# Moving the rotation of queries and keys of a two-layer attention block from VectorE to GpSimd

## The reference

```python
qa = rope_2d(rmsnorm(qa.reshape(B, S, A_HEADS, HEAD_DIM), q_norm_a[e]), grid_row, grid_col)
ka = rope_2d(rmsnorm(ka.reshape(B, S, A_KV, HEAD_DIM), k_norm_a[e]), grid_row, grid_col)
ya = global_gqa(qa, ka, va.reshape(B, S, A_KV, HEAD_DIM))

def rmsnorm(x, g):            # y = x * rsqrt(mean(x*x) + EPS) * g
def _rotate_axis(xa, ang):    # x1, x2 = halves of 16: [x1*c - x2*s, x1*s + x2*c]
```

## Time and profile before

| | us |
|---|---|
| median of 3 runs | 2544.85 |
| lowest and highest | 2544.52, 2552.52 |
| the profiled execution, its own time | 2547.12 |
| its span, first to last instruction | 2545.3 |
| TensorE busy | 2409.3 |
| VectorE busy | 1325.8 |
| ScalarE busy | 1209.5 |
| GpSimd busy | 864.6 |

### The profile page before, as it was taken

How to read it: one execution, slowest core, us unless ns; L and a number is a source line. 1 busy time by engine, 2 the same in 40 slices (tenths; PEclk the granted TensorE clock), 3 DMA queues, 4 the chain that set the end, 5 groups by cost and what they waited for, 6 DMA issues and landing times.

```text
span 2545.3 us, 36154 instructions
## 1 busy us (share of the span) xinstructions
PE 2409.3 (95%) x12568; PEld 2029.2 (80%) x12568; DVE 1325.8 (52%) x2734; ACT 1209.5 (48%) x2873; POOL 864.6 (34%) x1063
## 2 busy tenths in 40 slices
PE   7999888999999999999999999998899999999999
PEld 6878677878887878888888887776678888888877
DVE  7444667666776423345655555676766303322321
ACT  6444455556675434455656555554554213322331
POOL 5433111111225642221222222567665323222322
PEclk9999999999999999999999999999999999999999
DMA  6312101111234242222222323422233211111112
GB/s 216 111 55 67 30 26 26 30 36 32 62 93 127 85 132 63 88 70 86 87 79 81 88 87 120 142 75 76 70 87 94 66 49 46 49 50 47 50 50 87
DMA packets 305844, 191.92 MB, mean 75 GB/s; under 512 B 63744, under 2 KB 284160, under 8 KB 305152
## 3 DMA queue, kind: packets, MB, share of 16 engines
q1 hardware_dynamic: 305664, 189.61, 25.2%
HBM read 170.16 MB, written 19.40 MB: 74 GB/s over the span
## 4 chain that ended last, share of the span: by engine, by line
PE 79%; DVE 9%; issue 5%; ACT 4%; POOL 3%; DMA 1%; SPq 0%; DVEq 0%; POOLq 0%; ACTq 0%
PE PS L1464 21%; PE PS L1466 20%; PE PS L1465 20%; PE PS L1610 5%; PE PS L1577 4%; PE PS L1564 2%; PE PS L1565 2%; PE PS L1621 2%; POOL WS L2295 1%; ACT PY L1699 1%; DVE ST L2046 1%; ACT PT L1699 1%; DVE PY L2120 1%; ACT EO L1699 1%; DVE QKV L1920 1%
## 5 line engine op out<-in xcount | busy, mean ns | idle before, releaser
L2295 POOL TENSOR_TENSOR WS<-WR,WS 128x256 fp32r<-128x256 f32 (+1 forms) x939 | 726.2, 792 | 1565.9 <-ACT WS L1699 1564.8
L1464 PE MATMUL PS<-HT,WS 128*128 128x512 f32 x2080 | 839.3, 404 | 37.2 <-POOL WS L2295 18.0
L1466 PE MATMUL PS<-HT,WS 128*128 128x512 f32 x2080 | 816.9, 393 | 0.0
L1465 PE MATMUL PS<-HT,WS 128*128 128x512 f32 x2080 | 816.5, 393 | 0.0
L1699 ACT ACTIVATE WS<-WR 128x256 fp32r<-128x256 f32 (+1 forms) x954 | 355.3, 408 | 375.4 <-PE PS L1466 342.8
L1464 PEld LDWEIGHTS PS<-HT,WS 128*128 128x128 f32 x2080 | 394.7, 190 | 134.2 <-issue 33.3
L1466 PEld LDWEIGHTS PS<-HT,WS 128*128 128x128 f32 x2080 | 393.9, 189 | 84.7
L1465 PEld LDWEIGHTS PS<-HT,WS 128*128 128x128 f32 x2080 | 395.2, 190 | 74.4
L1699 ACT ACTIVATE PT<-PS 128x512 fp32r<-128x512 f32 x352 | 186.1, 529 | 242.8 <-PE PS L1577 242.4
L1920 DVE TENSOR_TENSOR PT<-PS,PT 128x512 fp32r<-128x512 f32 x352 | 208.4, 608 | 92.1 <-ACT PT L1699 90.8
L1610 PE MATMUL PS<-PT,QKV 128*128 128x256 f32 (+1 forms) x1248 | 210.9, 291 | 12.5 <-DVE YB L2110 11.7
(11 more groups left out here) (176 smaller groups left out, 2908.1 us busy)
## 6 DMA issues: line engine op xcount, KB each, us to landing
WR<-in_ffn_in SPq DMA_DIRECT2D x120, 256.0 KB, 2.9
WR<-in_w_in_odd SPq DMA_DIRECT2D x106, 256.0 KB, 3.0
EO<-in_grid SPq DMA_DIRECT2D x48, 384.0 KB, 3.1
WR<-in_w_in_even SPq DMA_DIRECT2D x100, 128.0 KB, 2.6
WR<-in_w_out_odd SPq DMA_DIRECT2D x48, 256.0 KB, 2.9
yd<-PY SPq DMA_DIRECT2D x44, 256.0 KB, 3.2
WR<-in_w_in_even SPq DMA_DIRECT2D x34, 256.0 KB, 2.9
WR<-in_w_out_even SPq DMA_DIRECT2D x64, 128.0 KB, 2.8
```

Source lines behind the costliest of these rows:

```text
L1464: e.matmul(out, wh, rh, start=start, stop=False)
L1465: e.matmul(out, wh, rl, start=False, stop=False)
L1466: return e.matmul(out, wl, rh, start=False, stop=stop)
L2295: e.tensor_tensor(WS[:, i % NSPL, 1, 0:n], RAW[raw_slot(u)][:, o:o + n], f32(WS[:, i % NSPL, 0, 0:n]), ALU.subtract).then_inc(s_wlop.sem, 1)
```

## The change

Rope 2 and rope 3 are dealt out anew. GpSimd makes, as rope 2, all that was in either except for the product with the root: gain, four sine products, cosines, sum, seven operations on a semaphore of its own (`s_rp`). VectorE keeps the sum of squares (rope 1) and, as rope 3, makes the product with the root, which now comes last. F1 is free after GpSimd's first operation. Rope 3 is put one yield later. GpSimd makes the root of rope 1 first, as before, since that stands ahead in the list.

```diff
             yield False
-            h.vd2 = s_ed.n
-            s_ed.add(6)
-            f1["after"] = (s_ed, h.vd2 + 1)
+            h.vp2 = s_rp.n
+            s_rp.add(7)
+            f1["after"] = (s_rp, h.vp2 + 1)
             put("rope 2", h)
             at["f1"] = False
             yield False
-            h.vd3 = s_ed.n
-            s_ed.add(2)
+            yield False
+            h.vd3 = s_ed.add()
             put("rope 3", h)
             yield True
...
                 elif kind == "rope 4":
                     h, = of
-                    w.wait_ge(s_ed, h.vd3 + 2)
+                    w.wait_ge(s_ed, h.vd3)
...
-                elif kind == "rope 2":
...
                 elif kind == "rope 3":
                     h, = of
-                    a4 = RA.rearrange("p (t h f) -> p t h f", t=4, h=2)
-                    w.wait_ge(s_ed, h.vd2 + 6)
-                    e.tensor_tensor(a4, a4, COS[:, 4 * h.n:4 * h.n + 4, :].unsqueeze(2).to_broadcast([128, 4, 2, 64]), ALU.mult).then_inc(s_ed.sem, 1)
-                    w.wait_ge(s_ed, h.vd3 + 1)
-                    e.tensor_tensor(RA, RA, RBUF, ALU.add).then_inc(s_ed.sem, 1)
+                    a3 = RA.rearrange("p (g f) -> p g f", f=64)
+                    w.wait_ge(s_rs, h.vp)
+                    w.wait_ge(s_rp, h.vp2 + 7)
+                    e.tensor_tensor(a3, a3, SS[:, 8:16].unsqueeze(2).to_broadcast([128, 8, 64]), ALU.mult).then_inc(s_ed.sem, 1)
...
+                elif kind == "rope 2":
+                    h, = of
+                    gi = h.to[4]
+                    a3, x3 = RA.rearrange("p (g f) -> p g f", f=64), F1[:, :].rearrange("p (g f) -> p g f", f=64)
+                    w.wait_ge(s_ea, h.va + 2)
+                    w.wait_ge(s_ed, h.vd + 1)
+                    w.wait_ge(d_tab, 64)
+                    e.tensor_tensor(a3, x3, GQ[:, gi:gi + 1, :].to_broadcast([128, 8, 64]), ALU.mult).then_inc(s_rp.sem, 1)
...
+                    w.wait_ge(s_rp, h.vp2 + 1)
+                    for hh in range(2):
+                        for s in range(2):
+                            e.tensor_tensor(b5[:, :, hh, :, s, :], a5[:, :, hh, :, 1 - s, :], t5[:, :, :, s, :], ALU.mult).then_inc(s_rp.sem, 1)
+                    w.wait_ge(s_rp, h.vp2 + 5)
+                    e.tensor_tensor(a4, a4, COS[:, 4 * h.n:4 * h.n + 4, :].unsqueeze(2).to_broadcast([128, 4, 2, 64]), ALU.mult).then_inc(s_rp.sem, 1)
+                    w.wait_ge(s_rp, h.vp2 + 6)
+                    e.tensor_tensor(RA, RA, RBUF, ALU.add).then_inc(s_rp.sem, 1)
```

More of the change, by code:

```diff
@@ L277, in build @@
         s_whi, s_wlop, s_wlov, s_wused = (signal(n) for n in ("s_whi", "s_wlop", "s_wlov", "s_wused"))
-        s_mm, s_ea, s_ed, s_flip, s_rs = (signal(n) for n in ("s_mm", "s_ea", "s_ed", "s_flip", "s_rs"))
+        s_mm, s_ea, s_ed, s_flip, s_rs, s_rp = (signal(n) for n in ("s_mm", "s_ea", "s_ed", "s_flip", "s_rs", "s_rp"))
         s_score, s_mx, s_exp, s_sink, s_rec = (signal(n) for n in ("s_score", "s_mx", "s_exp", "s_sink", "s_rec"))
@@ L2310, in gpsimd_program @@
                     root(SS, 0, 8, 8).then_inc(s_rs.sem, 1)
+                elif kind == "rope 2":
[6 more added lines that the diff above has]
+                    e.tensor_tensor(a3, x3, GQ[:, gi:gi + 1, :].to_broadcast([128, 8, 64]), ALU.mult).then_inc(s_rp.sem, 1)
+                    a5 = RA.rearrange("p (t h x s f) -> p t h x s f", t=4, h=2, x=2, s=2)
+                    b5 = RBUF.rearrange("p (t h x s f) -> p t h x s f", t=4, h=2, x=2, s=2)
+                    t5 = SIN[:, 4 * h.n:4 * h.n + 4, :].rearrange("p t (x s f) -> p t x s f", x=2, s=2)
+                    a4 = RA.rearrange("p (t h f) -> p t h f", t=4, h=2)
+                    w.wait_ge(s_rp, h.vp2 + 1)
[6 more added lines that the diff above has]
+                    e.tensor_tensor(RA, RA, RBUF, ALU.add).then_inc(s_rp.sem, 1)
                 elif kind == "nsplit lo":
```

## The result

| | before | changed |
|---|---|---|
| median of the runs, us | 2548.71 (5 runs, 2544.52 to 2552.52) | 2535.14 (5 runs, 2531.48 to 2536.05) |
| the profiled execution, its own time | 2547.12 | 2536.05 |
| its span | 2545.3 | 2534.2 |

The ratio is 0.9946, with a 95% interval of 0.993 to 0.9963: 13.6 us or 0.54% faster in the medians, 11.1 us in the two profiled executions. Forecast were 2535 us and a gain of 9.7 us. So the time came out as forecast while the gain was some 4 us larger than forecast, and the base some 4 us higher: two misses that cancel.

The account below looks back on a forecast made before the run. TensorE holds 79% of the chain, so time lies only in its idle or lower-clock stretches. 7.1 + 5.7 - 2.8 - 0.3 = 9.7 us gained, giving 2535 us from the median 2544.85; 8-in-10 range 2530 to 2547.

Parts of the forecast that it names:

- The price on GpSimd: Seven rotation operations in each half, priced like GpSimd's subtractions: 5.7 us, 5.9 with three handovers.
- The warning end: GpSimd's power, 1.64 us for 8 columns, kept only as a warning that the operations might cost more than subtractions.
- Part 1: Global attention, six halves q05:0 to q07:1: rotation leaves VectorE's queue ahead of the score's maximum; 7.1 us gained.
- the cover of the kept product: Global attention: VectorE's 0.69 us product fits in 1.03 us before the exponential starts; without cover 0.7 us each.
- Part 2: ka:1: v's turning passes rope 4, removing waits of 2.22 and 4.26 us; net 5.7 us gained.
- 2.0 us of half clock: ka:1: TensorE's slow stretch at 191 to 198 us goes with the waits, worth 2.0 us.
- Part 3: q04:1: TensorE waits for rope 1 to 4, GpSimd's longer chain counting 1:1; 2.8 us lost.
- (c): Rival: TensorE's clock falls elsewhere; longer q04:1 hole keeps 6 us more at half clock, 3 us lost; chance 0.12.
- Part 4: ka:0 and q04:0, beside memory attention: low parts covered by 1.3 and 0.2 us; 0.3 us lost before q04:0's rope 4.
- (a): Rival: GpSimd operations cost more than subtractions, nearly 4 us per us over 5.9; no gain at 1.5 times; chance 0.18.
- (b): Rival: passing in ka:1 doesn't pay, the 4.26 us only move; gain there 2 us or less; chance 0.15.
- (d): Rival: more comes back than counted, VectorE also leaving rope 3's turn (1.8 us each); 2529 to 2531; chance 0.07.

Follow-up runs that it names:

- e10: Changed kernel without the extra step, GpSimd also making the product with the root as eighth operation: 2542.12 us, ratio 0.9974 to before.
- e2: Changed kernel without the extra step, rope 3 at its old place: 2554.51 us, ratio 1.0033 to before.
- e12: Changed kernel unchanged, run again on the chip of the versions it is compared with: 2535.31 us, ratio 0.9943 to before.
- e5: Only q05, q06 and q07 rotated the new way, ka and q04 as in the kernel before: 2537.29 us, ratio 0.9955 to before.
- e7: Changed kernel with one more 512-column operation in GpSimd's chain in each half: 2540.35 us, ratio 0.9969 to before.
- e4: Changed kernel with q04:1 alone back on VectorE, product with the root last: 2532.87 us, ratio 0.9945 to before.
- e6: Only ka and q04 rotated the new way, q05 to q07 as in the kernel before: 2548.86 us, ratio 0.9996 to before.
- e3: Changed kernel with q04:1 alone back on VectorE in the old order, root first: 2533.72 us, ratio 0.9949 to before.
- e11: Changed kernel with q04:1 on VectorE, root last, and GpSimd making the product too in the nine other halves: 2531.30 us, ratio 0.9923 to before.
- e1: Kernel before with the extra step alone, all rotation still on VectorE: 2547.95 us, ratio 0.9998 to before.
- e8: Changed kernel with three more 512-column operations in GpSimd's chain in each half: 2546.11 us, ratio 0.9987 to before.
- e13: The program of e4 again, on the same chip as the changed kernel's rerun: 2532.19 us, ratio 0.9931 to before.

## Why the prediction was right, and where it was not

**The price on GpSimd: right.** 5.65 us a half against 5.7, the handovers 0.07 to 0.08 us each, the whole from 255.88 to 261.60. The warning end, the power, had nothing to do with it. The product with the root cost GpSimd 1.04 us in e10, less than the subtraction. The product that VectorE kept was the term that I priced too low: 0.68 to 0.69 us in five halves, as forecast, but 0.90 to 1.14 in the five where GpSimd worked beside it (L2009, mean 839 ns). In q04:1, where it counts in full, it was 0.69.

The Trainium skill (GPSIMD Engine Reference, "Performance versus the Vector engine") says to leave such work to VectorE. The rows agree on its factor, 1.29 us against 0.69, and e2 shows a kernel for which the advice would have been right. The Trainium skill (GPSIMD Engine Reference, "Performance pitfalls for Q7 kernels") has half as much again for an SBUF input with an inner step over 8 bytes. The innermost step here is 4 bytes, so by its letter nothing was due, and no such surcharge is seen in the 0.43 us (1.70 for four) of the products in runs of 16; a step over 8 bytes is in no run here.

**Part 1: the mechanism right, the size too small.** The waits came out as forecast: 0.38 and 0.38 (forecast 0.4), 0.92 (0.9), the 0.42, 0.42 and 1.32 gone. TensorE's waits in the stretch fell by 8.7 us, not 7.1: I had not counted the small ones that go with them, 0.47 to 0.49 us in front of L1610 in three halves, now 0.30 to 0.32, 0.32 us at 522, now gone, and 1.33 us at 348, now 0.77 (0.58 in e12). At equal half clock the stretch became 10.5 us shorter (e5, e12); of the 1.8 us beyond the waits some 0.6 can be put down to the half clock, of which 1.3 us lay in waits and before none; where the rest came from isn't shown. In the execution that was profiled first, with 17.1 us of half clock, the stretch was 2.8 us longer, and so the changed kernel's own 7.7 us look like a hit of 7.1. They are one by chance.

The step of this part that was thin is the cover of the kept product. I wrote that without it 0.7 us each would be lost. e2 shows that the cover is the extra step and that its price is not the product's length but VectorE's wait: 2.99 + 1.13 us ahead of the maximum in q05:0. Of the 8.7 us of waits that went in the changed kernel only 0.8 went in e2.

**Part 2: the waits right, the net between 4.0 and 6.0 us.** 2.22 and 4.26 went, 2.41 came (2.45 forecast), the slow stretch of 191 to 198 went. The low part that I gave 0.3 us cost 0.12; e7 shows that it stood right at the edge. But behind the 2.45 us in ka:0, which hasn't changed, there is now half clock that the trace of before doesn't have:

```profile
172.00:178.00 6.00, 5.97 (x21) 4.87 (x22) 2.24 (x7) 1.33 (x5) 0.73 (x1) 0.72 0.01 3
```

In e4 and e6, the same program up to there, it fell behind the wait at 201 instead. From the 17th to the 25th maximum before took 58.65 us and the changed kernel 54.63 (54.62 in e12): 4.0 us, not 5.7, as if 1.7 of the "2.0 us of half clock" that go had come back. But e5, whose ka is rotated as before, has that fall too, at 172.2 us, beside the 6.8 us of half clock at 192.7, and took 60.62 us: against it part 2 gave 6.0. So the half clock of 191 to 198 did go, and whether some comes back at the waits of 2.45 us differs between executions: once in the changed kernel, e12, e3, e4, e6 and e11, twice in e1, e7, e8 and e13, which cost e13 another 1.6 us beside e4. The term is not refuted; what it lacks is that spread. What I didn't see is that this part hangs on the other engine: the step alone (e1) has 0.77 us to pay in ka:1 and 1.33 in q04:0, the engine alone (e2) lengthens the waits in ka:1 from 6.48 to 8.58.

**Part 3: the wait right, its cost between half and whole.** 10.1 us forecast, 9.98 measured. Between the 29th and the 33rd maximum 1.4 us were lost against the trace of before, not 2.8, and e3 gained 1.4 us by taking 2.65 us of wait away; against e5, with its shorter half clock, 2.6 us were lost. The step that failed in the first two comparisons is "that stretch shifts, and I take its length as unchanged": its length was unchanged, 10.2 us, but it didn't shift with the end of the wait, it had begun in the wait. Rival (c) expected more half clock after a longer hole; there was none more in the changed kernel. e10, e7 and e8 (13.7 us of half clock from the hole on, after 10.36, 11.09 and 13.34 us of wait) show it after longer ones, and e4, e13 and e11 (6.8, 6.8 and 3.4 us after 5.6) less after shorter ones.

**Part 4: right.** No wait for a low part in ka:0, none over 0.15 us in q04:0; 0.16 us in front of q04:0's rope 4 where 0.3 was taken. e8 measured ka:0's cover: 3.4 us more gave 1.69 us of wait, so 1.7 us were covered, against 1.3.

**The sum.** Early 2.2 us (2.6), global attention 7.7 to 10.5 (7.1), with the rest of the kernel untouched but for the clock: 1983.9 and 1986.1 us against 1984.7. That is 10 to 13 us by the traces, and 13.6 by the medians, against 9.7. The forecast time was met to 0.1 us because the base of three runs, 2544.85, lay 4 us under the one of five and the gain was 4 us above the sum: that closeness is luck. The term that was sized too small is part 1, 8.7 us of waits and up to 10.5 us of time for 7.1.

**The rivals.** (a) was excluded by the first row of the new operations; its slope was near right, 2.7 us for the first 1.1 and 11.0 for 3.4. (b), the passing doesn't pay, is refuted for the changed kernel. Of the two halves of the change e2 has no passing and longer waits; in e1 the passing took 3.3 us of waits away up to the 25th maximum, so (b)'s mechanism wasn't there either. (c) did not come in the hole of q04:1; the 6.8 us more of half clock in the first profile's global attention were not there in e12. (d) came in small, as the small waits of part 1. VectorE's busy time fell by 33.8 us, a little under the 35 to 38 named.

## What to carry to other kernels

When work moves to a helper engine, price first where the old engine will stand waiting for it and what is queued behind, and only then the operations: the same seven operations gave 7 us lost or 14 us won, and the difference was one step by which the last product was put later. Test the engine and the order of such a change together, since neither alone (e2, e1) showed the gain. And where a helper's result stands between two idle stretches of the main engine, use the engine that is free at that point; in q04:1 that was VectorE, with the slow root made beside it and applied last.

## What the runs showed of the hardware that I had not expected

- The amount of TensorE's half clock differs between executions of one program: 10.2 and 17.1 us of it in the same 52 maxima of the changed kernel, at equal waits, for 276.2 and 279.0 us. This goes far to make the spread of the runs. The 53 runs of before beside the experiments (2543.0 to 2553.7 us) each have a mean granted clock on record, and time goes with it: the six at 0.981 took 2553.1 us at the mean, the six at 0.986 2543.9. At 0.985 fourteen runs of before took 2546.8 at the mean and four of the changed kernel 2534.2, so at an equal clock the gain was 12.6 us.
- A longer idle time doesn't always cost its length when the clock falls in it anyway: 2.65 us of wait were worth 1.4 us between e3 and the changed kernel, but the same difference was worth 2.6 us between e5 and the changed kernel.
- GpSimd's products of 512 columns with gain or cosines as the second operand took 1.26 to 1.31 us in seventeen of twenty cases and 1.54 to 1.56 in three, and 1.04 us with the eight roots of a row (e10, ten of them between 1.037 and 1.052) or with the first operand twice (e7, e8). Why these are shorter wasn't tried.
- VectorE's product with two operands in SBUF took 0.69 us alone and up to 1.14 us while GpSimd worked (rows at 261.70 and 189.43), while its low part from a bank took 0.69 us in both cases (in e10 between 143 and 530 us, 28 of them with GpSimd busy beside them had a mean of 0.690 us, 62 with GpSimd idle 0.692). It goes the other way too: in e4 the root took GpSimd 2.02 us beside VectorE's products, in place of 1.63. That a shared way to SBUF is the cause wasn't tried.
